# Expert rows summed on VectorE instead of TensorE, in a two-layer hybrid backbone with a product-key expert stage

## The chip, the cores and the metric

The kernel runs on one core of a Trainium2 chip. The metric is the device time of one execution in microseconds. The core has five instruction streams that run beside each other and meet at semaphores: TensorE (PE, with its weight loads PEld), VectorE (DVE), ScalarE (ACT), GpSimd (POOL) and SyncE (SP).

## The reference

The reference is one inference step over two layers for 128 prompt tokens and 512 sample tokens, 640 in all, with 1024 channels, in fp32. Each layer mixes tokens (three mixers and an attention) and then channels. The change touches only the second half of the channel mixing, the expert retrieval:

```python
s = jnp.einsum('thsk,snk->thsn', q, sub_keys)            # 8 heads, 2 sides, 128 keys
sv, si = lax.top_k(s, PEER_TOPK)                          # best 16 of each side
cand_s = sv[..., 0, :, None] + sv[..., 1, None, :]        # 256 sums
top_s, top_pos = lax.top_k(cand_s, PEER_TOPK)             # best 16 of them -> idx, g = softmax(top_s)

def block(args):                                          # 128 tokens, 128 experts a token
    tb, ib, gb = args
    a = jax.nn.gelu(jnp.einsum('tkd,td->tk', jnp.take(u_tab, ib, axis=0), tb))
    return jnp.einsum('tk,tkd->td', gb * a, jnp.take(v_tab, ib, axis=0))
```

So each token has 8 x 16 = 128 experts. For each, a row U of 1024 numbers is fetched and multiplied with the token (a dot product), the result goes through gelu and is weighted with the gate g, and a row V of 1024 numbers, scaled by that weight, is added to the token's output. Both tables hold 16,384 rows a layer, in device memory.

## The kernel before, in words

**Tiles.** The 640 tokens are five tiles of 128, one token a partition. In the expert stage, tile after tile, GpSimd fetches for expert n of all 128 tokens at once one U row each and one V row each by an indirect DMA: 128 x 4 KB = 512 KB a gather, 256 gathers a tile, 1280 a layer, 1342 MB in the whole kernel.

**Slots.** Four slots hold U rows and four hold V rows (`rows_u`, `rows_v`, in the ring that holds the weights in other stages). A gather waits until the slot is free (`rows_u_free`, `rows_v_free`; `gather`, L1600). GpSimd works in order: first the 16 U rows of a tile's first head, then U row n and V row n-16 in turn (`later_heads`, L1618), because the weight of a V row is only known when its head's 16 dot products are done. The last V rows of a tile are mixed with the first U rows of the next. The tile's indices stand in one buffer, `idx_u`; the last head's are copied to `idx_last` (`pass_last`), and the next tile's are put into `idx_u` (`pass_indices`, L1439) once VectorE has seen the V rows before them come in.

**VectorE** does a dot product per expert (`dot_products`, L1510; a multiply and sum of 128x1024 and a read of the accumulator). After 16 of them it drains and signals ScalarE, which takes the gelu of the 16 values (L1087). VectorE then builds 16 diagonal matrices for the head before (`diagonals`, L1498): the identity times activation times gate, 128x128 each, with two sets of 16 for two heads. Between groups of four dot products it does a part of the selection for the next tile (`select_part`, L1458: best keys of two heads at a time, pair sums, best sums, positions, indices, gates), in heads 2 to 7 of a tile. In the last tile of a layer there is no following one, and so no selection.

**TensorE** multiplies each diagonal with its V row and accumulates all 128 experts of a tile in PSUM, in two halves of 512 columns (L822); fp32 makes two passes of each, so four matmul records a row. At the end of the tile ScalarE copies the sum to SBUF, TensorE turns it (eight transposes, L830), and VectorE adds it, times the gate g2, to the residual (`add_output`, L1488). TensorE also computes the next tile's key scores and turns the next tile's tokens, from a staging buffer that ScalarE fills.

**Order.** The instructions of each engine are written out by hand. PSUM accumulators are handed on in a fixed order of turns (`turn_table`, L81). The layers are a hardware loop on every engine, and so are most tiles; inside such a loop the value of a wait is computed in registers.

Of the kernel before, what the change touches and what calls it, by code (L numbers as in the profile page):

```python
# [75 lines left out]
ROWS_U, ROWS_V = 4, 4  # L76
LAST = EXPERTS - TOPK
# [3 lines left out]
def turn_table():  # L81
# [8 lines left out]
    order += [("pq", n) for n in range(2 * PH)] + [("key", 0), ("key", 1), "tok"]  # L90

    for j in range(TILES - 1):
        names = [("next_key", 0), ("next_key", 1), "next_tok", "peer_out"]
        order += names if j == 0 else [(name, j) for name in names]
    order += ["peer_last"]
# [55 lines left out]
def build(nc, x_prompt, x_sample, cache_ckv, cache_kpe, c, c_ctx, w_ada, b_ada, norm1, norm2, w_in,  # L151
# [4 lines left out]
    with ExitStack() as ctx:  # L156
# [44 lines left out]
        g2_cur = sb("g2_cur", [P, KC])  # L201
# [42 lines left out]
        pq_t = view(0, 2 * PH, T)  # L244
# [19 lines left out]
        idx_u, idx_v = kt_flat[:, 0:P].bitcast(U32), kt_flat[:, 4 * P:5 * P].bitcast(U32)  # L264
        g_cur = kt_flat[:, P:2 * P]
        dots, acts = kt_flat[:, 2 * P:3 * P], kt_flat[:, 3 * P:4 * P]
        idx_last = idx_v[:, 0:TOPK]
        idx_next, g_next = kt_flat[:, 5 * P:6 * P].bitcast(U32), kt_flat[:, 6 * P:7 * P]
        ring_flat = ring[:].rearrange("p s n -> p (s n)")
        rows_u = ring_flat[:, 0:ROWS_U * D].rearrange("p (s n) -> p s n", s=ROWS_U)  # L270
        rows_v = ring_flat[:, ROWS_U * D:(ROWS_U + ROWS_V) * D].rearrange("p (s n) -> p s n", s=ROWS_V)
        diag = [m_flat[:, n * TOPK * P:(n + 1) * TOPK * P].rearrange("p (k n) -> p k n", k=TOPK) for n in range(2)]
        tok_cur = m_flat[:, 4096:4096 + D]
        stage = cv_flat[:, 2048:2048 + D].rearrange("p (k n) -> p k n", k=KC)
        y_tok = uq[:].rearrange("p k h n -> p (k h n)")[:, 0:D]
# [71 lines left out]
        last_ready = signal("last_ready", TILES)  # L347
        tok_ready = signal("tok_ready", TILES)
        stage_ready = signal("stage_ready", 3 * (TILES - 1))
        y_full = signal("y_full", TILES)  # L350
# [6 lines left out]
        diag_ready = signal("diag_ready", TILES * PH)  # L357
        ytok_ready = signal("ytok_ready", TILES)
# [19 lines left out]
        def _(sp):  # L378
# [18 lines left out]
            with sp.Fori(0, LAYERS) as l:  # L397
# [41 lines left out]
        def _(pe):  # L439
# [62 lines left out]
            with pe.Fori(0, LAYERS) as l:  # L502
# [278 lines left out]
                def key_scores(name, n, more, queries):  # L781

                    a = open_turn(l, name, more)
                    for g in range(PH):
                        mm = pe.matmul(a[:, g * P:(g + 1) * P], queries[:, g, :], turned[:, 4 + g % 2, :],  # L785
                                       start=True, stop=True)
                    close_turn(name, mm)

                def tokens(name, more, tile):

                    a = open_turn(l, name, more)
                    for k in range(KC):
                        mm = pe.transpose(a[:, k * P:(k + 1) * P], tile[:, k, :], ident)
                    close_turn(name, mm)

                for n in range(2):
                    key_scores(("key", n), n, 0, pq_t[:, n * PH:(n + 1) * PH, 0:P])
                tokens("tok", 0, h_t[:, :, 0:P])

                def staged(j, n):  # L800

                    pe.wait_ge(stage_ready.sem, stage_ready.after(l, n + 1) + j * 3)

                def peer_tile(j, out, more, following):


                    for h in range(PH):
                        if following and h < 2:
                            staged(j, h)
                            key_scores(("next_key", h), h, j * 2, stage)  # L810
                        if following and h == H_TOK + 1:
                            staged(j, 2)
                            tokens("next_tok", j * 2, stage)
                        pe.wait_ge(diag_ready.sem, diag_ready.after(l, h + 1) + j * PH)
                        for k in range(TOPK):
                            n = h * TOPK + k
                            s = n % ROWS_V
                            pe.wait_ge(rows_v_in[s].sem,
                                       rows_v_in[s].after(l, 16 * (n // ROWS_V + 1)) + j * (16 * EXPERTS // ROWS_V))
                            for half in range(2):  # L820
                                cols = slice(half * 512, (half + 1) * 512)
                                mm = pe.matmul(y_acc[:, cols], diag[h % 2][:, k, :], rows_v[:, s, cols],  # L822
                                               start=n == 0, stop=n == EXPERTS - 1)
                            mm.then_inc(rows_v_free.sem, 1)
                    pe.drain().then_inc(y_full.sem, 1)
                    a = open_turn(l, out, more)

                    pe.wait_ge(ytok_ready.sem, ytok_ready.after(l, 1) + j)
                    for k in range(KC):
                        mm = pe.transpose(a[:, k * P:(k + 1) * P], y_tok[:, k * P:(k + 1) * P], ident)  # L830
                    close_turn(out, mm)

                with pe.Fori(0, TILES - 1) as j:
                    peer_tile(j, "peer_out", j * 2, True)
                peer_tile(TILES - 1, "peer_last", 0, False)
# [21 lines left out]
        def _(act):  # L857
# [40 lines left out]
            with act.Fori(0, LAYERS) as l:  # L898
# [151 lines left out]
                with act.Fori(0, 2) as i:  # L1050
                    for n in range(8):
                        a = full(l, ("pq", n), i * 4)
                        act.copy(arena[:, bass.ds(i * (8 * T) + n * T, T)], a[:, 0:T]).then_inc(pq_ready.sem, 1)
                        act.wait_ge(pq_ready.sem, pq_ready.after(l, n + 1) + i * 8)
                        act.sem_inc(give_back(("pq", n)), 1)

                def soft(j):

                    act.wait_ge(soft_in.sem, soft_in.after(l, 1) + j)
                    act.activation(best_e, best_e, ACT.Exp).then_inc(soft_exp.sem, 1)  # L1060

                def take_tokens(name, more, j):

                    a = full(l, name, more)
                    act.copy(tok_cur, a[:, 0:D]).then_inc(tok_ready.sem, 1)
                    act.wait_ge(tok_ready.sem, tok_ready.after(l, 1) + j)
                    act.sem_inc(give_back(name), 1)

                def put_stage(src):
                    act.copy(stage, src).then_inc(stage_ready.sem, 1)  # L1070

                def queries(j, n):

                    return pq_t[:, n * PH:(n + 1) * PH, bass.ds(j * P, P)]

                def peer_tile(j, following):
                    for h in range(PH):
                        if following and h == 0:
                            put_stage(queries(j + 1, 0))
# [42 lines left out]
        def _(dve):  # L1122
# [28 lines left out]
            with dve.Fori(0, LAYERS) as l:  # L1151
# [306 lines left out]
                def select_part(j, h, quarter):  # L1458
# [26 lines left out]
                    elif at == (6, 3):  # L1485
                        gates(j + 1)
# [245 lines left out]
```

## Time and profile before

| | |
|---|---|
| three executions, us | 6154.2, 6157.3, 6170.8; median 6157.3 |
| span of the profiled execution, us | 6172.5 |
| time of the profiled execution itself | not recorded apart from these; its span lies at the slowest of the three |
| busy: PE, PEld, DVE, ACT, POOL, us | 4637.5, 2050.5, 2873.5, 450.7, 2863.0 |
| read from device memory | 1484 MB, of which the gathers 1342 MB |
| mean granted TensorE clock | 0.938 |

Times in the rows are microseconds from the start of the span, unless marked ns; L12 is line 12 of the kernel before. An engine's busy time holds no register, branch or semaphore work and no waiting. GpSimd's gathers are busy while their descriptors are made; the transfers themselves then run on 16 DMA engines. The ends of matmuls are modelled. In a timeline, the bracket at the end of a row is the time for which the engine was idle before it, and what ended that.

### The profile page before, as it was taken

The numbers are of one execution on the slowest core, as the hardware profiler recorded it, in microseconds if no ns is written. First come the engines' busy times: TensorE is split into PE (matmuls) and PEld (weight loads), VectorE is DVE, ScalarE is ACT, GpSimd is POOL, SyncE is SP. The second block draws the span as 40 slices with busy tenths as digits, with TensorE's granted clock in tenths as the row PEclk, the third lists the DMA queues.
The fourth block names the chain that finished last, engine by engine and source line by source line (L and its number), as shares of the span: only waits on it lengthen the run. The fifth ranks groups of instructions, "written<-read, shape, count | busy, mean of one in ns | idle before, by whom it ended". The sixth has DMA issues, their size and how long they took to land.

```text
span 6172.5 us, 45021 instructions
## 1 busy us (share of the span) xinstructions
PE 4637.5 (75%) x12847; PEld 2050.5 (33%) x12847; DVE 2873.5 (47%) x6890; ACT 450.7 (7%) x830; POOL 2863.0 (46%) x2569
## 2 busy tenths in 40 slices
PE   7999996566666766667789999956676766666666
PEld 3645544122222222222245555532222222222222
DVE  2241113665656656545312411146657566565543
ACT  1131010000000000000010400100000000000000
POOL 0000000676776767777500000017767777677774
PEclk9999998899999999999999999978999999999999
DMA  7101110899999999999851012119999999999996
GB/s 231 55 28 36 60 55 14 318 346 340 339 353 330 337 333 331 348 332 368 310 170 63 21 43 66 48 45 325 352 343 333 339 329 339 340 335 354 345 354 245
DMA packets 504201, 1489.50 MB, mean 241 GB/s; under 512 B 49632, under 2 KB 172976, under 8 KB 502578
## 3 DMA queue, kind: packets, MB, share of 16 engines
q0 software_dynamic: 368640, 1342.34, 59.6%
q1 hardware_dynamic: 126000, 140.54, 7.1%
q10 hardware_dynamic: 9346, 4.38, 0.3%
q8 instruction: 58, 0.95, 0.1%
q14 instruction: 157, 1.29, 0.1%
HBM read 1484.30 MB, written 2.79 MB: 241 GB/s over the span
## 4 chain that ended last, share of the span: by engine, by line
PE 39%; DMA 24%; issue 18%; DVE 9%; POOL 7%; ACT 1%; DVEq 1%; POOLq 0%; another core or an unknown queue 0%; PEldq 0%; PEld 0%; ACTq 0%; SPq 0%
DMA ring<-in_peer_v_dram,kt 16%; PE ps L468 10%; PE ps L822 10%; DMA ring<-in_peer_u_dram,kt 7%; POOL ring L1605 7%; PE ps L747 7%; DVE m_t L1506 3%; PE ps L511 2%; PE ps L754 2%; DVE ring L1517 2%; PE ps L552 1%; PE ps L699 1%; PE ps L679 1%; PE ps L627 1%; PE ps L499 1%
## 5 line engine op out<-in xcount | busy, mean ns | idle before, releaser
L822 PE MATMUL ps<-ring,m_t 128*128 128x512 f32 x5120 | 2655.2, 651 | 1270.3 <-DMA ring<-in_peer_v_dram,kt 913.1
L1605 POOL DMA_INDIRECT ring<-in_peer_u_dram,kt x1280 | 1363.8, 1065 | 2742.0 <-issue 1447.6
L1517 DVE CUSTOM_DVE_ANT_0 ring<-ring,m_t 128x1024 f32<-128x1024 f32 x1280 | 1553.7, 1225 | 1465.9 <-DMA ring<-in_peer_u_dram,kt 1403.3
L822 PEld LDWEIGHTS ps<-ring,m_t 128*128 128x128 f32 x5120 | 940.1, 201 | 2969.5 <-DMA ring<-in_peer_v_dram,kt 1797.0
L1605 POOL DMA_INDIRECT ring<-in_peer_v_dram,kt x1280 | 1498.6, 1171 | 519.1 <-issue 286.3
L468 PE MATMUL ps<-h_t,ring 128*128 128x128 f32 (+1 forms) x1536 | 426.1, 438 | 21.9 <-ACT h_t L895 14.6
L747 PE MATMUL ps<-h_t,ring 128*128 128x128 f32 (+1 forms) x1536 | 425.1, 435 | 11.7 <-issue 9.1
L1506 DVE TENSOR_SCALAR m_t<-cst,kt 128x128 f32<-128x128 f32 x1280 | 343.8, 367 | 21.5 <-issue 11.6
L468 PEld LDWEIGHTS ps<-h_t,ring 128*128 128x128 f32 x1536 | 235.1, 192 | 214.6 <-issue 209.7
L747 PEld LDWEIGHTS ps<-h_t,ring 128*128 128x128 f32 x1536 | 235.4, 191 | 199.6 <-issue 199.6
L1087 ACT ACTIVATE kt<-kt 128x16 f32<-128x16 f32 x80 | 17.3, 216 | 3439.7 <-DVEq L1533 1905.6
L511 PE MATMUL ps<-ring,cond_t 128*2 128x256 f32 x768 | 176.3, 383 | 31.9 <-issue 19.5
L1337 DVE TENSOR_TENSOR arena<-arena,ps 128x512 f32<-128x512 f32 x64 | 28.3, 484 | 336.6 <-ACT arena L1043 336.6
L1361 DVE MAX8 zc<-ps 128x8 f32<-128x128 f32 x160 | 38.2, 286 | 307.5 <-PE ps L785 290.1
L468 PE MATMUL ps<-m_t,ring 128*128 128x128 f32 (+1 forms) x512 | 143.8, 442 | 7.6 <-DVEq L1341 6.1
L511 PEld LDWEIGHTS ps<-ring,cond_t 128*2 128x2 f32 x768 | 62.4, 85 | 145.2 <-issue 56.0
L754 PE MATMUL ps<-cv,ring 128*128 128x128 f32 (+1 forms) x384 | 109.1, 434 | 0.0
L552 PE MATMUL ps<-ring,h_t 128*128 128x256 f32 (+1 forms) x480 | 98.5, 366 | 14.0 <-ACT h_t L895 14.0
L1156 DVE COPY arena<-ps 2x256 f32 x48 | 19.8, 412 | 186.0 <-PE ps L511 186.0
L1517 DVE DVE_READ_ACCUMULATOR2_ANT kt<- 128x1 f32 x1280 | 105.6, 83 | 0.0
L468 PEld LDWEIGHTS ps<-m_t,ring 128*128 128x128 f32 x512 | 79.1, 193 | 72.4 <-issue 72.4
L1337 DVE TENSOR_TENSOR m_t<-arena,ps 128x512 f32 (+1 forms) x32 | 14.2, 484 | 187.1 <-ACT arena L1043 187.1
(212 smaller groups left out, 2592.1 us busy)
## 6 DMA issues: line engine op xcount, KB each, us to landing
ring<-in_w_ada_dram SPq DMA_DIRECT2D x48, 1024.0 KB, 6.7
ring<-in_w_in_dram SPq DMA_DIRECT2D x36, 1024.0 KB, 5.4
ring<-in_peer_u_dram,kt POOLq DMA_INDIRECT x1280
ring<-in_peer_v_dram,kt POOLq DMA_INDIRECT x1280
ring<-in_peer_wq_dram SPq DMA_DIRECT2D x16, 1024.0 KB, 5.5
ring<-in_tables_dram SPq DMA_DIRECT2D x10, 1024.0 KB, 4.8
ring<-in_w_out_dram SPq DMA_DIRECT2D x8, 1024.0 KB, 5.0
ring<-in_w_branch_c_dram SPq DMA_DIRECT2D x8, 512.0 KB, 6.5
```

The lines of the kernel that those rows point to most:

```text
L468: mm = pe.matmul(a[:, lo:hi], lhs[k], rhs[k][:, lo:hi], start=k == 0, stop=k == n - 1)
L499: mm = pe.matmul(a[:, lo:hi], mean_w[:], m_t[:, k, lo:hi], start=k == 0, stop=k == KC - 1)
L511: mm = pe.matmul(a[0:2, 0:CW], cond_t[:, 0:2, k], w[:, k, :], start=k == 0, stop=k == KC - 1)
L552: mm = pe.matmul(a[:, at:at + n], h_t[:, k, j * P:(j + 1) * P], w[:, k, 0:n], start=k == 0, stop=k == KC - 1)
L627: mm = pe.matmul(a[:, at:at + 512], big[:, j, q * P:(q + 1) * P], hy[:, j, lo:lo + 512], start=j == 0, stop=j == STILES - 1)
L679: mm = pe.matmul(a[:, at:at + hi - lo], q_t[:, h, j * P:(j + 1) * P], k_h[h % 2][:, lo:hi], start=True, stop=True)
L747: pe.matmul(a[:, at_g:at_g + hi - lo], wg[:, k, cols], h_t[:, k, lo:hi], start=k == 0, stop=k == KC - 1)
L754: mm = pe.matmul(a[:, at_y:at_y + hi - lo], wb[:, (0, 2, 4)[b] + k, cols], y_k[b][k][:, lo:hi], start=k == 0, stop=k == n - 1)
L822: mm = pe.matmul(y_acc[:, cols], diag[h % 2][:, k, :], rows_v[:, s, cols], start=n == 0, stop=n == EXPERTS - 1)
L1506: ins = dve.tensor_scalar(diag[h % 2][:, k, :], ident, acts[:, n:n + 1], g_cur[:, n:n + 1], ALU.mult, ALU.mult)
L1517: dve.tensor_tensor_reduce(rows_u[:, s, :], rows_u[:, s, :], tok_cur, 1.0, 0.0, ALU.mult, ALU.add, dots[:, n:n + 1]).then_inc(rows_u_free. ...
L1605: pool.indirect_dma_start(rows[:, s, :], None, table, bass.IndirectOffsetOnAxis(ap=idx, axis=0)).then_inc(came[s].sem, 16)
```

## The change

It does five things.

1. The weighted sum of V rows moves to VectorE. `diagonals` and the matmuls with them go. `make_weights` multiplies activation and gate for a head; `add_row` waits for a V row, does `y = row * weight + y` over 128x1024 in SBUF, drains, and frees the slot. `add_row` of expert n-16 stands directly before the dot product of expert n. The sum is complete in SBUF, so ScalarE's copy of it goes too; TensorE still turns it.
2. There are eight V slots in place of four; the new four stand where the diagonals were.
3. Indices and gates have two buffers, by the parity of the tile; `pass_indices` and `pass_last` go, with the wait for V rows.
4. The tile loops and the layer loops are unrolled on all engines; waits have constants. GpSimd goes straight on from one tile to the next.
5. ScalarE's staging copies go, since TensorE can address every tile's data directly; for this the queries `pq_t` are laid out by tile. The output addition of a tile stands in the next tile after the second quarter of its fourth head, no longer after its first head.

```diff
-ROWS_U, ROWS_V = 4, 4
+ROWS_U, ROWS_V = 4, 8
...
-                def diagonals(j, h):
-                    if h >= 2:
-                        dve.wait_ge(rows_v_free.sem, rows_v_free.after(l, (h - 1) * TOPK) + j * EXPERTS)
-                    dve.wait_ge(acts_ready.sem, acts_ready.after(l, h + 1) + j * PH)
-                    for k in range(TOPK):
-                        n = h * TOPK + k
-                        ins = dve.tensor_scalar(diag[h % 2][:, k, :], ident, acts[:, n:n + 1],
-                                                g_cur[:, n:n + 1], ALU.mult, ALU.mult)
-                    ins.then_inc(diag_ready.sem, 1)
+                def make_weights(j, h):
+                    cols = slice(h * TOPK, (h + 1) * TOPK)
+                    dve.wait_ge(acts_ready.sem, acts_ready.after(l, j * PH + h + 1))
+                    dve.tensor_tensor(wts[:, cols], acts[:, cols], g_of[j % 2][:, cols], ALU.mult)
+                    dve.drain()
+
+                def add_row(j, n):
+                    s, y = n % ROWS_V, y_sums[:, j % 2, :]
+                    dve.wait_ge(rows_v_in[s].sem, rows_v_in[s].after(l, 16 * ((j * EXPERTS + n) // ROWS_V + 1)))
+                    if n == 0:
+                        dve.tensor_scalar(y, rows_v[s], wts[:, n:n + 1], None, ALU.mult)
+                    else:
+                        dve.scalar_tensor_tensor(y, rows_v[s], wts[:, n:n + 1], y, ALU.mult, ALU.add)
+                    last = dve.drain()
+                    last.then_inc(rows_v_free.sem, 1)
+                    if n == EXPERTS - 1:
+                        dve.sem_inc(y_ready.sem, 1)
...
                 def dot_products(j, h, k0, k1):
                     for k in range(k0, k1):
                         n = h * TOPK + k
+                        if n >= TOPK:
+                            add_row(j, n - TOPK)
+                        elif j:
+                            add_row(j - 1, n + EXPERTS - TOPK)
                         s = n % ROWS_U
...
+                for j in range(TILES):
+                    dve.wait_ge(tok_ready.sem, tok_ready.after(l, j + 1))
+                    for h in range(PH):
+                        if h:
+                            make_weights(j, h - 1)
+                        elif j:
+                            make_weights(j - 1, PH - 1)
+                        for quarter in range(4):
+                            if j + 1 < TILES:
+                                select_part(j + 1, h, quarter)
+                            dot_products(j, h, quarter * TOPK // 4, (quarter + 1) * TOPK // 4)
+                            if j and (h, quarter) == (3, 1):
+                                add_output(j - 1)
+                        dve.drain().then_inc(dots_ready.sem, 1)
+                make_weights(TILES - 1, PH - 1)
+                for n in range(EXPERTS - TOPK, EXPERTS):
+                    add_row(TILES - 1, n)
+                add_output(TILES - 1)
...
+                for j in range(TILES):
+                    for n in range(EXPERTS):
                         u_row(j, n)
+                        if n >= TOPK:
+                            v_row(j, n - TOPK)
+                        elif j:
+                            v_row(j - 1, n + EXPERTS - TOPK)
+                for n in range(EXPERTS - TOPK, EXPERTS):
+                    v_row(TILES - 1, n)
```

## Rows read from the trace of the kernel before

**Rows 1.** The page's slices: busy share of the DMA engines in tenths, 154 us each.
```profile
DMA  7101110899999999999851012119999999999996
```
**Rows 2.** The page's chain of waits, shares of the span by engine.
```profile
PE 39%; DMA 24%; issue 18%; DVE 9%; POOL 7%; ACT 1%; DVEq 1%; POOLq 0%; another core or an unknown queue 0%; PEldq 0%; PEld 0%; ACTq 0%; SPq 0%
```
**Rows 3.** Busy time by stretches: one steady tile of the first layer.
```profile
core 0: us, PE busy (x) PEld busy (x) DVE busy (x) ACT busy (x) POOL busy (x), PEclk, DMA share, GB/s
1458.00:1849.00 391.00, 267.68 (x558) 97.65 (x559) 243.05 (x599) 12.11 (x18) 285.17 (x255) 0.95 0.93 341
```
**Rows 4.** Groups by line, 1458 to 1849 us: busy us, mean ns; idle before.
```profile
L1605 POOL DMA_INDIRECT ring<-in_peer_v_dram,kt x127 | 149.2, 1175 | 47.4 <-issue 30.4 <-PE ps L822 13.5 <-remote 3.5
L1605 POOL DMA_INDIRECT ring<-in_peer_u_dram,kt x128 | 136.2, 1064 | 58.4 <-issue 33.8 <-DVE kt L1517 20.1 <-PE ps L822 4.5
L1506 DVE TENSOR_SCALAR m_t<-cst,kt 128x128 f32<-128x128 f32 x115 | 31.0, 369 | 2.0 <-issue 1.2 <-ACT kt L1087 0.7
```
**Rows 5.** Timeline of GpSimd: start, us, what, idle before.
```profile
1710.59 2.66 POOL L1605 DMA_INDIRECT ring<-in_peer_v_dram,kt  x1 [0.30 <-issue]
...
1716.16 1.98 POOL L1605 DMA_INDIRECT ring<-in_peer_v_dram,kt  x1 [0.30 <-issue]
...
1734.40 0.94 POOL L1605 DMA_INDIRECT ring<-in_peer_v_dram,kt  x1 [0.30 <-issue]
```
**Rows 6.** Timeline of VectorE at the same time, columns alike.
```profile
1710.15 2.28 DVE L1413 TENSOR_TENSOR cv<-zc,cst 128x2048 f32<-128x2048 f32 x1
1712.67 1.23 DVE L1517 CUSTOM_DVE_ANT_0 ring<-ring,m_t 128x1024 f32<-128x1024 f32 x1 [0.23 <-issue]
...
1714.97 1.22 DVE L1517 CUSTOM_DVE_ANT_0 ring<-ring,m_t 128x1024 f32<-128x1024 f32 x1
...
1716.12 1.22 DVE L1517 CUSTOM_DVE_ANT_0 ring<-ring,m_t 128x1024 f32<-128x1024 f32 x1
```
**Rows 7.** Timeline of VectorE around two drains, one with an increment.
```profile
629.12 0.89 DVE L1337 TENSOR_TENSOR arena<-arena,ps 128x512 f32<-128x512 f32 x2 [11.64 <-ACT arena L1043]
630.12 0.83 DVE L1340 TENSOR_TENSOR m_t<-m_t,arena 128x640 f32 x1
...
1079.09 2.29 DVE L1428 TENSOR_REDUCE zc<-cv 128x128 f32<-128x2048 f32 x1
1081.45 0.29 DVE L1433 SCALAR_TENSOR_TENSOR zc<-zc 128x128 f32<-128x128 f32 x1
```
**Rows 8.** Timeline of VectorE: the first instruction of four tiles.
```profile
1083.79 0.23 DVE L1524 COPY kt<-kt 128x128 f32<-128x128 f32 x1 [0.55 <-issue]
...
1458.45 0.33 DVE L1524 COPY kt<-kt 128x128 f32<-128x128 f32 x1
...
2652.52 0.23 DVE L1524 COPY kt<-kt 128x128 f32<-128x128 f32 x1
...
5716.30 0.23 DVE L1524 COPY kt<-kt 128x128 f32<-128x128 f32 x1
```
**Rows 9.** Timeline of VectorE: the first op after the first head.
```profile
1118.01 0.17 DVE L1537 COPY g_cur<-g_all 128x8 f32<-128x8 f32 x1
```
**Rows 10.** Timeline of VectorE: parts of the selection.
```profile
1047.64 0.29 DVE L1376 CAST zc<-zc 128x256 f32<-128x256 uint32 x1
...
1512.67 0.48 DVE L1361 MAX8 zc<-ps 128x8 f32<-128x128 f32 x2
...
1515.58 1.21 DVE L1517 CUSTOM_DVE_ANT_0 ring<-ring,m_t 128x1024 f32<-128x1024 f32 x1
```
**Rows 11.** Timeline of all engines at the second layer's end.
```profile
6092.99 0.08 DVE L1517 DVE_READ_ACCUMULATOR2_ANT kt<- 128x1 f32 x1
...
6093.47 4.26 DVE L1506 TENSOR_SCALAR m_t<-cst,kt 128x128 f32<-128x128 f32 x16 [0.40 <-ACT kt L1087]
...
6134.06 2.16 DVE L1493 SCALAR_TENSOR_TENSOR x_t<-ps,g_cur,x_t 128x128 f32<-128x128 f32 x8 [36.33 <-PE ps L830]
...
6154.51 6.46 DVE L1583 SCALAR_TENSOR_TENSOR h_t<-x_t,cond_t,root 128x640 f32<-128x640 f32 x8
```

More of the change, by code:

```diff
@@ L89, in turn_table @@
     order += [("gate", n) for n in range(3 * KC)] + [("out", n) for n in range(KC)] + ["norm2"]
[L90 to L95, printed above, removed]
+    order += [("pq", n) for n in range(2 * PH)] + [("key0", 0), ("key1", 0), ("tok", 0)]
+    for j in range(TILES):
+        if j + 1 < TILES:
+            order += [("key0", j + 1), ("key1", j + 1)]
+        if j:
+            order += [("peer_out", j - 1)]
+        if j + 1 < TILES:
+            order += [("tok", j + 1)]
+    order += [("peer_out", TILES - 1)]
     assert len(order) % 2 == 0, len(order)
@@ L395, in cols_of @@
                 return w[l, :, bass.ds(start, n)].rearrange("(k p) n -> p k n", p=P)
-            with sp.Fori(0, LAYERS) as l:
+            for l in range(LAYERS):
                 with sp.Fori(0, N_ADA // SLOTS) as i:
@@ L500, in root_mean @@
                 close_turn(name, mm)
-            with pe.Fori(0, LAYERS) as l:
+            for l in range(LAYERS):
                 pe.wait_ge(cond_ready, 2)
@@ L786, in key_scores, with tokens @@
                                        start=True, stop=True)
                     close_turn(name, mm)
-                def tokens(name, more, tile):
-                    a = open_turn(l, name, more)
+                def tokens(j):
+                    a = open_turn(l, ("tok", j))
                     for k in range(KC):
[L793 to L797, printed above, removed]
@@ L896, in add_shift @@
                                    bias=mod[:, shift + k, 1:2], scale=amp[:, which, k, 1:2]).then_inc(h_ready.sem, 1)
-            with act.Fori(0, LAYERS) as l:
+            for l in range(LAYERS):
                 def put(dst, src):
@@ L1049, in _ @@
                 add_shift(l, KC, 3 * KC)
[L1050 to L1055, printed above, removed]
+                for n in range(2 * PH):
+                    a = full(l, ("pq", n))
+                    act.copy(pq_t[:, :, n, :], a[:, 0:T].rearrange("p (j n) -> p j n", j=TILES))\
+                        .then_inc(pq_ready.sem, 1)
+                    act.wait_ge(pq_ready.sem, pq_ready.after(l, n + 1))
+                    act.sem_inc(give_back(("pq", n)), 1)
@@ L1149, in normalise @@
                     dve.tensor_tensor(h_t[:, k, :], x_t[:, k, :], rinv[:, :], ALU.mult).then_inc(scaled.sem, 1)
-            with dve.Fori(0, LAYERS) as l:
+            for l in range(LAYERS):
                 with dve.Fori(0, N_ADA // SLOTS) as i:
@@ L1350, in _, with best_keys @@
                 normalise(l, 1)
[L1353 to L1355 removed]
+                def best_keys(j, n, g0, g1):
+                    name = (f"key{n}", j)
+                    a = full(l, name)
                     carry_waits(dve, "dve")
@@ L1598, in _ @@
             pool.sem_inc(rows_v_free.sem, ROWS_V)
-            def gather(rows, idx, free, came, table, l, j, n, slots):
-                s = n % slots
-                pool.wait_ge(free.sem, free.after(l, n + 1 - slots) + j * EXPERTS)
-                carry_waits(pool, "pool")
-                pool.indirect_dma_start(rows[:, s, :], None, table, bass.IndirectOffsetOnAxis(
-                    ap=idx, axis=0)).then_inc(came[s].sem, 16)
             u_rows, v_rows = (w.rearrange("l n d -> (l n) d") for w in (peer_u, peer_v))
-            with pool.Fori(0, LAYERS) as l:
+            for l in range(LAYERS):
```

233 lines of the change are left out of this document (73 added, 160 removed).

## The prediction

> **What bounds the kernel now.** The slices of the page come first: the DMA digits stand at 9 in two long stretches, slices 9 to 19 and 28 to 39, and nowhere else for long [rows 1]. These are the expert stages of the two layers; the change works there. The chain of waits gives 39% to TensorE, 24% to DMA, 18% to "issue" [rows 2]: no engine owns the end, so the stage has to be read from inside.
>
> The table by stretches shows a tile with a following tile: 391 us hold 285.2 us of GpSimd in 255 gathers, 243 of VectorE, 268 of TensorE; DMA share 0.93 at 341 GB/s [rows 3]. Each gather has 0.30 us of "issue" ahead of it [rows 5], so GpSimd is occupied for 285.2 + 255 x 0.30 = 362 of 391 us. It is the nearest thing to a bound, with the DMA engines behind it. A gather of V rows takes 1.175 us in the mean and one of U rows 1.064 [rows 4], 2.84 us a pair with the issue time. Its shortest form is 0.94 [rows 5]; the long ones have a cause that can be read. The gather at 1710.59 took 2.66 us and VectorE's two-input op had begun at 1710.15 and ended at 1712.43; the one at 1716.16 took 1.98 under a dot product ending at 1717.34 [rows 5, 6]. Both end 0.8 us after the VectorE op does: a gather that starts under a VectorE op with two SBUF inputs is held until that op ends. The diagonals, with one tensor input, are 0.369 us each and 31 us of that stretch [rows 4].
>
> The cadence: tiles open at 1083.8, 1458.5 and 2652.5 (three tiles between the last two, 398.0 us each), and in the second layer the last one at 5716.3 [rows 8]. The last tile has no selection in it and takes until 6093.1, so 376.8 us, 47.1 us a head; then 43.1 us pass to the end of the last output addition (6134.06 + 2.16) [rows 8, 11].
>
> **The change part by part.**
>
> *Removed*: 1280 x 4 fp32 matmul passes on TensorE, off the path except at the end, and 128 diagonals a tile, 31 to 34 us of VectorE [rows 4] in a VectorE that now idles 148 of 391 us [rows 3].
>
> *Added*: on VectorE, for every expert, a multiply-add of 128x1024 and a drain. The nearest row is the dot product, same size, two SBUF inputs: 1.22 us, and 1.15 from start to start when nothing holds it (1714.97 to 1716.12) [rows 6]. The final scaling, the same operation at 640 columns, takes 6.46/8 = 0.81 us [rows 11], which fits one element per 1.04 ns. I take 1.22. The gap after a drain is 0.07 us alone (1081.38 to 1081.45), 0.11 with a semaphore increment (630.01 to 630.12) [rows 7], and 0.24 where a wait with a register value follows (1712.43 to 1712.67) [rows 6]. The new drain has an increment, and a wait on a constant behind it: 0.17, between the last two. So add 1.39, dot 1.15, **2.54 us a pair**; bounds 2.48 and 2.61.
>
> A head of 16 pairs costs 40.6 us, and 0.8 for its weights: the last dot of a head to VectorE's next instruction is 0.40 us, by way of ScalarE [rows 11], plus one small op and two drains. 41.4 us.
>
> *Selection* is as before but now lies in a VectorE without slack. Two heads of key scores take 1512.67 to 1515.58, 2.9 us, eight times a tile [rows 10]; the rest takes 35.6 us (1047.64 to 1083.24) [rows 8, 10]. By heads: 11.6 in the second and third, 12.5 in the fourth, 7.1, 9.5 and 6.5 in the next three. The output addition (2.2 us and drains, 2.6) falls into the fourth.
>
> A head is then the longer of VectorE's work and the supply of rows. For the supply I take the last tile's 47.1 us a head (2.9 us a pair), the only stretch without selection. The lower bound is VectorE's own pace; the upper is under rival B.
>
> - Steady tile: 47.1 + 53.0 + 53.0 + 56.5 + 50.6 + 50.9 + 49.5 + 47.1 = 407.7 (the fifth and seventh are 48.5 and 47.9 of VectorE, and 2.1 and 1.6 for their last pairs, which outrun the supply); plus 1.9 for the hand-over (the wait for the turned tokens, today behind the last diagonals); less 4, the rows landed ahead when the seventh head ends. 405.6 against 398.0: +7.6, three times, **+22.8**.
> - First tile: 34.2 for the U rows alone (1083.8 to 1118.0 [rows 8, 9]), then 53.0, 53.0, 53.9, 50.6, 50.9, 49.5, 43.1 and 1.9: 390.1 against 374.7. **+15.4**.
> - Last tile: supply, no change. **0**, between -33 (rival C) and +34 (rival B).
> - Tail: today 43.1 us, in which TensorE works off 16 rows at its own pace. Then: weights 0.8, 16 x 1.39 = 22.2, eight transposes on a cold TensorE and the hand-overs 2.3, the addition 2.2: 27.5. **-15.6**.
>
> Sum: +22.6 a layer, **+45 us**. The profiled execution has a span of 6172.5 us and lies at the top of the three times (6154 to 6171), so its rows may be 0.2% long; I set the sum on the median 6157 and get 6202, in round numbers **6200 us**.
>
> *Edits priced at nothing.* Eight V slots: GpSimd issues U row n+4 and then V row n-12 in order, and U row n+4 waits for dot n. When it waits there, the adds stand at n-16, so four V rows are out and the other four slots are unused; they matter only in the tail, where V rows run ahead. Unrolling: the same instructions run, with constants in place of register values; its only price is in the drain gap above. Double-buffered indices take away a lull at each hand-over (a wait for the last V rows); it is in the supply's spare time as long as VectorE is the longer, and if it is not, it gives back up to 3 us a tile. The pq copies go to strided places, once a layer, and the staging copies of ScalarE go: both beside other work.
>
> The Trainium skill speaks against this change: "SBUF — State Buffer", in its text on the shared port pair and on "DVE blocks DMA", says that VectorE with two SBUF inputs locks out a GpSimd op that reads SBUF, and that a gather's descriptors wait meanwhile. The trace agrees (0.8 us after the op's end, above); by it, what it leads to is rival B. The same page lets a one-input op in a two-port mode lock too; the diagonals are the candidates here, and gathers that begin under them are not visibly held. "VectorE: DVE Perf Modes", section on the DRAIN that can't be avoided, finds that semaphores after each op cost nothing extra; by that a pair would be 2.30 us and the steady tile some 20 us shorter. Rows 6 and 7 show 0.07 to 0.24 beyond the op's end, so I go by them.
>
> **The rivals.**
>
> *B, slower: GpSimd loses to the port.* Today the 128 dots cover 128 x 1.22 = 156 of 391 us, 40%, and the gathers are 0.18 us over 0.94 in the mean [rows 4], so some 0.4 where one is hit, the selection's long ops left aside. With adds, two-input ops cover 2.44 of 2.9 us, 84%. Hit at random, a gather pays 0.84 x 0.4 = 0.34, a pair 2 x (0.94 + 0.30 + 0.34) = 3.16 us, 51.3 us a head with the weights. This decides as soon as it exceeds the 47.1 above. Steady tile 423 (four heads at 51.3 or a little over, the rest as above), first 404, last 411, tail 27.5: 2112 against 374.7 + 1194 + 376.8 + 43.1 = 1989 a layer, +123, in all **6400 us**. Against it: a held gather goes through at the next op boundary, 0.8 + 0.3 us later the next one starts, and an op lasts 1.15 to 1.39. So GpSimd may fall into step, one gather for each VectorE op, and then costs nothing over 2.54 a pair. Both held gathers of the rows let the current op end and no further one [rows 5, 6].
>
> *C, faster: the supply improves.* Without the lull, in step, with the drain gap at 0.11 (pair 2.48) and rows every 2.64 us (400 GB/s): a head without selection takes 43.0 us and VectorE's own 40.5. Steady 391 (-7, three times), first 380 (+5), last 344 (-33), tail 26 (-17). That is 66 us a layer less, **6025 us**. For it: GpSimd unhindered needs 2.48 a pair. Against: the stretches never show more than 341 GB/s.
>
> *D, the slots do it:* if eight V slots really deepened the queue, the supply would be better than in C but VectorE's own sum for a steady tile (8 x 41.4 + 58.8 + 2.6 + 1.9 = 394.5) would still stand; nearly C's time, and counted there.
>
> **How the numbers follow.** Forecast (VectorE and the supply near balance, 6200, own range 6145 to 6260): 0.48. B (6260 to 6400 and over): 0.23. C (6020 to 6140): 0.27. Left over 0.02. About 0.3% (18 us) is what can be told from no change. Faster by more: all of C and a little of the forecast's lower end, 0.29. Same: 0.15. Slower: 0.56. The range 6050 to 6370 leaves out the ends of B and C.
>
> **What would show it.** Right: the multiply-add at 1.22 us and its successor 0.17 later; VectorE above 85% busy in heads with selection, its idle time in the first, last and light heads waiting for DMA; tiles at 405; tail 27. B: gathers at 1.3 us and longer in the mean, steady tiles over 415, VectorE idle in every head. C: DMA share over 0.95, last tile under 360. Wrong altogether: a drain that costs more than 0.3 us (each 0.1 is 10 us a tile), or an add over 1.3.

## The result, and the profile after

The changed kernel takes **6275.1 us** (median of four runs, 6267.6 to 6281.8), the kernel before 6155.8 (four runs): ratio **1.0213** [1.0179 to 1.0246]. The forecast was 6200, so the sign was right and the size was not: +119 us in place of +45. The spans of the two profiled executions, 6280.0 and 6172.5, differ by 107.5.

The page after: busy times, the DMA digits of the 40 slices, the chain's shares, and three groups (busy us, mean ns | idle before). They answer to [rows 1, 2, 4].

```profile
PE 2023.4 (32%) x7727; PEld 1142.2 (18%) x7727; DVE 4134.0 (66%) x6930; ACT 393.5 (6%) x779; POOL 2811.5 (45%) x2569
...
DMA  7101110899899898899951011118998998989997
...
DVE 35%; PE 29%; issue 15%; POOL 12%; DMA 6%; DVEq 2%; ACT 1%; POOLq 0%; PEldq 0%; PEld 0%; SPq 0%; ACTq 0%
...
L1547 POOL DMA_INDIRECT ring<-in_peer_u_dram,kt x1280 | 1441.4, 1126 | 3002.2 <-DVE kt L1392 2165.9
L1476 DVE CUSTOM_DVE_ANT_0 ring<-ring,m_t 128x1024 f32<-128x1024 f32 x1280 | 1568.0, 1225 | 233.7 <-issue 202.3
L1460 DVE SCALAR_TENSOR_TENSOR uq<-m_t,kt,uq 128x1024 f32<-128x1024 f32 x640 | 820.5, 1282 | 88.0 <-DMA m_t<-in_peer_v_dram,kt 78.1
```

VectorE's share of the chain goes from 9% to 35%, that of DMA from 24% to 6%: an engine that was hardly on the path now has the largest part of it. The DMA digits, all 9 inside the two expert stages before, fall to 8 in part. A multiply-add (L1460) lasts 1.282 us.

The timeline of VectorE in a steady tile, then GpSimd's beside it (start, us, what, idle before).

```profile
1603.04 1.28 DVE L1460 SCALAR_TENSOR_TENSOR uq<-m_t,kt,uq 128x1024 f32<-128x1024 f32 x1
1604.48 1.23 DVE L1476 CUSTOM_DVE_ANT_0 ring<-ring,m_t 128x1024 f32<-128x1024 f32 x1 [0.16 <-issue]
1605.63 0.08 DVE L1476 DVE_READ_ACCUMULATOR2_ANT kt<- 128x1 f32 x1
1605.63 1.28 DVE L1460 SCALAR_TENSOR_TENSOR uq<-m_t,kt,uq 128x1024 f32<-128x1024 f32 x1
```

```profile
1603.93 1.20 POOL L1547 DMA_INDIRECT ring<-in_peer_u_dram,kt  x1 [3.01 <-DVE kt L1476]
1605.44 1.08 POOL L1556 DMA_INDIRECT ring<-in_peer_v_dram,kt  x1 [0.30 <-issue]
1606.82 0.94 POOL L1547 DMA_INDIRECT ring<-in_peer_u_dram,kt  x1 [0.30 <-issue]
1608.06 1.04 POOL L1556 DMA_INDIRECT ring<-in_peer_v_dram,kt  x1 [0.31 <-issue]
1609.41 0.94 POOL L1547 DMA_INDIRECT ring<-in_peer_u_dram,kt  x1 [0.30 <-issue]
```

From add to add are 2.59 us, of which 0.16 behind the drain. From U gather to U gather are also 2.59 (1606.82 to 1609.41): GpSimd has fallen into step, one gather for each VectorE operation, and few are held for long: between 1500 and 1860 us 134 of 222 gathers last over 1.00 us, 8 of them over 1.7. All 134 end 0.80 to 0.82 us after the end of a VectorE operation. So what the prediction read from two gathers holds for all of them.

Busy time by stretches: a steady tile, then the last tile of the first layer; they answer to [rows 3].

```profile
core 0: us, PE busy (x) PEld busy (x) DVE busy (x) ACT busy (x) POOL busy (x), PEclk, DMA share, GB/s
1490.00:1880.00 390.00, 7.72 (x32) 6.63 (x32) 354.31 (x594) 4.38 (x10) 260.44 (x243) 0.50 0.91 324
2740.00:3090.00 350.00, 1.94 (x8) 1.57 (x8) 297.29 (x371) 1.51 (x7) 271.39 (x238) 0.50 0.97 357
```

VectorE is busy 91% of the steady stretch (62% before), and the core moves 324 GB/s there (341 before). TensorE's granted clock reads 0.50, the lower of its two levels (1.2 GHz), with 7.7 us of work in 390; nothing waits for it but the end of a tile.

The first dot products of tiles 1, 2, 3 and 5 and the tail of the first layer, on VectorE and TensorE; they answer to [rows 8, 11].

```profile
1088.50 1.23 DVE L1476 CUSTOM_DVE_ANT_0 ring<-ring,m_t 128x1024 f32<-128x1024 f32 x1 [4.58 <-DMA ring<-in_peer_u_dram,kt]
...
1485.63 1.23 DVE L1476 CUSTOM_DVE_ANT_0 ring<-ring,m_t 128x1024 f32<-128x1024 f32 x1 [0.16 <-issue]
...
1897.30 1.22 DVE L1476 CUSTOM_DVE_ANT_0 ring<-ring,m_t 128x1024 f32<-128x1024 f32 x1 [0.16 <-issue]
...
2727.62 1.23 DVE L1476 CUSTOM_DVE_ANT_0 ring<-ring,m_t 128x1024 f32<-128x1024 f32 x1 [0.16 <-issue]
...
3102.29 0.18 DVE L1449 TENSOR_TENSOR kt<-kt 128x16 f32<-128x16 f32 x1 [0.33 <-ACT kt L1050]
3102.55 5.50 DVE L1460 SCALAR_TENSOR_TENSOR uq<-ring,kt,uq 128x1024 f32<-128x1024 f32 x4
...
3119.39 5.50 DVE L1460 SCALAR_TENSOR_TENSOR uq<-m_t,kt,uq 128x1024 f32<-128x1024 f32 x4
...
3127.14 2.16 DVE L1440 SCALAR_TENSOR_TENSOR x_t<-ps,g_all,x_t 128x128 f32<-128x128 f32 x8 [2.25 <-PE ps L797]
```

Steady tiles take 414.0 us each (1485.63 to 2727.62, three tiles) against 398.0 [rows 8]. The same reading for both kernels, first dot to first dot (the last tile to its last dot, 3101.95), first layer, in us:

| | before | after | difference | forecast |
|---|---|---|---|---|
| first tile | 375.3 | 397.1 | +21.8 | +15.4 |
| three steady tiles | 1195.5 | 1242.0 | +46.5 | +22.8 |
| last tile | 367.6 | 374.3 | +6.7 | 0 |
| tail, to the end of the output addition | 43.2 | 27.4 | -15.8 | -15.6 |

That is +59.2 (forecast +22.6); the second layer, read alike, gives +18.3, +42.4, +6.2 and -15.8, so +51.1. Both together are 110.3 us, beside 107.5 between the spans. The heads of tile 2 in us, first dot to first dot (the forecast's 1.9 for the hand-over is put to the first head, its "less 4" to the eighth):

```
before    52.5  51.5  47.9  49.1  48.6  47.8  46.9  51.9
forecast  49.0  53.0  53.0  56.5  50.6  50.9  49.5  43.1
after     48.8  54.2  54.1  56.7  50.5  51.6  47.6  48.1
```

Heads 2 to 6 came out within 1.2 us of the forecast; the seventh is 1.9 below it and the eighth 5.0 above.

What GpSimd waited for around the last tile of the first layer (us in total, times, longest):

```profile
POOL ring L1547 <- issue: 36.6, 120, 0.3
POOL ring L1556 <- issue: 20.6, 63, 1.7
POOL m_t L1556 <- issue: 19.5, 64, 0.3
POOL ring L1547 <- DVE kt L1476: 6.7, 4, 2.5
POOL ring L1556 <- DVE kt L1476: 0.8, 1, 0.8
```

Nearly all of it is the 0.30 us of issue ahead of each gather. In the stretch from 2740 to 3090 us shown above, GpSimd is occupied for 271.4 + 238 x 0.30 = 343 of 350 us, and waits some 7 us for free slots. Its gathers take 1.14 us in the mean, 0.94 when nothing holds them. VectorE in turn waits 48 times for a V row there, 30 us in all.

### The profile page after: what moved, and what is told of

Same layout as the page of the kernel before. It is cut to its first block, busy times and chain, and to the rows that moved or that the text cites. A ratio compares the mean times of both kernels' runs of the same rounds, so it can differ in the third digit from the quotient of the medians.

```text
span 6280.0 us, 32515 instructions
## 1 busy us (share of the span) xinstructions
PE 2023.4 (32%) x7727; PEld 1142.2 (18%) x7727; DVE 4134.0 (66%) x6930; ACT 393.5 (6%) x779; POOL 2811.5 (45%) x2569
## 4 chain that ended last, share of the span: by engine, by line
DVE 35%; PE 29%; issue 15%; POOL 12%; DMA 6%; DVEq 2%; ACT 1%; POOLq 0%; PEldq 0%; PEld 0%; SPq 0%; ACTq 0%
DVE uq L1460 13%; DVE ring L1476 12%; PE ps L463 10%; POOL ring L1547 9%; PE ps L742 7%; DMA m_t<-in_peer_v_dram,kt 3%; PE ps L749 2%; PE ps L506 2%; POOL ring L1556 2%; POOL m_t L1556 1%; PE ps L547 1%; DMA ring<-in_peer_v_dram,kt 1%; PE ps L694 1%; DVE zc L1347 1%; PE ps L622 1%
## 5 line engine op out<-in xcount | busy, mean ns | idle before, releaser
L1547 POOL DMA_INDIRECT ring<-in_peer_u_dram,kt x1280 | 1441.4, 1126 | 3002.2 <-DVE kt L1392 2165.9
L1460 DVE SCALAR_TENSOR_TENSOR uq<-m_t,kt,uq 128x1024 f32<-128x1024 f32 x640 | 820.5, 1282 | 88.0 <-DMA m_t<-in_peer_v_dram,kt 78.1
L1460 DVE SCALAR_TENSOR_TENSOR uq<-ring,kt,uq 128x1024 f32<-128x1024 f32 x630 | 807.6, 1282 | 81.5 <-DMA ring<-in_peer_v_dram,kt 71.3
L1556 POOL DMA_INDIRECT ring<-in_peer_v_dram,kt x640 | 688.5, 1076 | 209.5 <-issue 207.4
L1556 POOL DMA_INDIRECT m_t<-in_peer_v_dram,kt x640 | 680.9, 1064 | 209.0 <-issue 206.3
L781 PE MATMUL ps<-turned,arena 128*128 128x128 f32 x320 | 67.9, 399 | 1736.7 <-ACTq L1043 1461.0
L797 PE MATMUL ps<-cst,uq 128*128 128x128 f32 x80 | 19.6, 426 | 1848.5 <-DVEq L1464 1335.3
L781 PEld LDWEIGHTS ps<-turned,arena 128*128 128x128 f32 x320 | 63.0, 302 | 1742.4 <-ACTq L1043 1463.2
L797 PEld LDWEIGHTS ps<-cst,uq 128*128 128x128 f32 x80 | 15.7, 223 | 1851.8 <-issue 1336.8
L506 PE MATMUL ps<-ring,cond_t 128*2 128x256 f32 x768 | 175.4, 382 | 30.7 <-issue 15.4
L789 PE MATMUL ps<-cst,h_t 128*128 128x128 f32 x80 | 19.7, 428 | 510.6 <-DVEq L1085 510.6
```

Source lines behind the costliest of these rows:

```text
L506: mm = pe.matmul(a[0:2, 0:CW], cond_t[:, 0:2, k], w[:, k, :], start=k == 0, stop=k == KC - 1)
L781: mm = pe.matmul(a[:, g * P:(g + 1) * P], pq_t[:, j, n * PH + g, :], turned[:, 4 + g % 2, :], start=True, stop=True)
L1460: dve.scalar_tensor_tensor(y, rows_v[s], wts[:, n:n + 1], y, ALU.mult, ALU.add)
L1547: pool.indirect_dma_start(rows_u[s], None, u_rows, bass.IndirectOffsetOnAxis(ap=idx_u[j % 2][:, n:n + 1], axis=0)).then_inc(rows_u_in[s].s ...
L1556: pool.indirect_dma_start(rows_v[s], None, v_rows, bass.IndirectOffsetOnAxis(ap=idx_u[j % 2][:, n:n + 1], axis=0)).then_inc(rows_v_in[s].s ...
```

## The experiments

**Theories**, with the numbers that the expectations use. 1: VectorE's own sum sets the tiles, and its add and drain are dearer than priced. 2: the supply of rows is what VectorE waits for, and the slots, GpSimd held at the port (the prediction's rival B) or the DMA engines set it. 3, named first with the run of eight U slots (e6): four U slots are too few to keep the rows coming while VectorE does a burst of other work, such as the selection. "Port" stands for the shared port pair that the prediction speaks of. The runs are called e1 to e11. Each ratio is to the kernel before, run on the same chip.

**The changed kernel again** (e9).

> The changed kernel itself, beside the two below on one chip, as the measure for the other experiments. All theories: 2.1% over the kernel before, as in its own comparison.

Measured 1.0221 [1.0203 to 1.0239], tiles 396.3, 411.5, 414.3, 414.0, 372.7, tail 27.3. The result stands.

**The drain behind each add taken away** (e1). A wait for the add before it stands ahead of each add instead.

```diff
+                    dve.wait_ge(rows_v_free.sem, rows_v_free.after(l, j * EXPERTS + n))
...
-                        dve.scalar_tensor_tensor(y, rows_v[s], wts[:, n:n + 1], y, ALU.mult, ALU.add)
-                    last = dve.drain()
-                    last.then_inc(rows_v_free.sem, 1)
+                        ins = dve.scalar_tensor_tensor(y, rows_v[s], wts[:, n:n + 1], y, ALU.mult, ALU.add)
+                    ins.then_inc(rows_v_free.sem, 1)
```

> Changed kernel; the drain after each multiply-add is replaced by a semaphore increment on the multiply-add itself and a wait for it ahead of the next one, a dot product later. Theory 1 (VectorE's serial time sets the tiles with selection): the 0.16 us gap behind every add goes, a pair takes 2.43 instead of 2.59 us, 2.6 us a head in the five heads a tile that VectorE holds at 50 to 57 us, 13 us a tile, eight such tiles: about 105 us less than the changed kernel, 6170 us. Theory 2 (the supply of rows, by slots and by GpSimd held at the port, sets them): under 25 us less, 6250 or more.

Measured 1.0165 [1.0149 to 1.0182], 6229.8 us: some 0.5% better, a third of what the pairs alone promise. VectorE, and GpSimd in the same tile:

```profile
1604.97 1.28 DVE L1461 SCALAR_TENSOR_TENSOR uq<-ring,kt,uq 128x1024 f32<-128x1024 f32 x1
1606.17 1.22 DVE L1477 CUSTOM_DVE_ANT_0 ring<-ring,m_t 128x1024 f32<-128x1024 f32 x1
1607.31 0.08 DVE L1477 DVE_READ_ACCUMULATOR2_ANT kt<- 128x1 f32 x1
1608.04 1.28 DVE L1461 SCALAR_TENSOR_TENSOR uq<-ring,kt,uq 128x1024 f32<-128x1024 f32 x1 [0.65 <-DMA ring<-in_peer_v_dram,kt]
```

```profile
1568.80 0.93 POOL L1557 DMA_INDIRECT ring<-in_peer_v_dram,kt  x1 [0.31 <-issue]
1570.04 1.96 POOL L1548 DMA_INDIRECT ring<-in_peer_u_dram,kt  x1 [0.30 <-issue]
...
1577.45 1.99 POOL L1557 DMA_INDIRECT ring<-in_peer_v_dram,kt  x1 [0.30 <-issue]
```

The dot product now starts 1.20 us after the add's start, not 1.44, so a pair is 2.34. But VectorE then waits for rows, 35 of 225 gathers between 1500 and 1860 us last over 1.7 us (8 of 222 in the changed kernel), and the mean over all rises from 1.10 to 1.17. So the port is a real limit. Of the 35 long gathers 17 began less than 0.1 us before an add's end, when the dot product had already begun, and ended 0.81 us after that dot product's end; the one at 1570.04 is an example. In the changed kernel, where the drain keeps the two operations apart, none of the eight long ones is of this kind.

**Four V slots in place of eight** (e2; `ROWS_U, ROWS_V = 4, 4`).

> Changed kernel with four V slots instead of eight. Theory 1 and the argument that GpSimd, in order behind U row n+4, never has more than four V rows out: no change in the tiles, up to 5 us a layer lost in the tail, 6275 to 6285. Rival (the eight slots deepen the queue): 20 us or more slower, over 6295.

Measured 1.0271 [1.0254 to 1.0289], 6294.3 us, more than was expected and just under the rival's 6295. Yet the tiles are as in the changed kernel (410.5, 414.2 and 411.4 for the steady ones, last 369.3), and the tails are 36.3 and 35.2 in place of 27.4 and 27.3. The eight slots act only where forecast, in the tail, but give 8 to 9 us a layer there: with four, adds wait up to 2.7 us for their row. The traces thus show 17 us of the 0.5% (31 us) between this ratio and e9's; the rest is within the two intervals.

**The selection left out of both kernels** (e3 the changed kernel, e4 the one before). In tiles 2 to 5 of each layer the best keys, pair sums, positions and indices are left out; each tile uses the indices of the first.

```diff
+                        dve.tensor_copy(idx_u[j % 2], idx_u[(j - 1) % 2]).then_inc(idx_ready.sem, 1)
```

> Changed kernel; the selection for the second to fifth tile of each layer is left out (they take the first tile's indices and gates). Theory 1: every tile falls to the last tile's 375 us from 412 to 415, the first by 25: some 145 us a layer, 5985 us. Theory 2 (supply sets the tiles): the selection is beside the supply, and under 60 us go in all.

> Kernel before, with the same selection left out. Theory 1 says that VectorE had 140 us of slack a tile there, so little is gained: heads fall from 48 or 49 to the last tile's 46, 10 us a tile, some 80 us in all, 6075. If selection were on the path in both kernels alike: 290 us less, 5865.

Measured 0.9767 [0.9747 to 0.9787] for the changed kernel and 0.9742 [0.9725 to 0.9758] for the one before. A stretch of a steady tile, changed kernel first:

```profile
1500.00:1800.00 300.00, 7.41 (x32) 6.42 (x32) 255.95 (x324) 4.17 (x9) 231.43 (x204) 0.51 0.96 355
```

```profile
1500.00:1800.00 300.00, 220.22 (x448) 80.46 (x448) 156.98 (x316) 5.21 (x10) 227.82 (x210) 0.96 0.98 367
```

The changed kernel's ratio is 5987 us, where theory 1 expected 5985. Without the selection the two ways of summing nearly cost the same. The surprise is the other half. The kernel before gains 161 us where 55 were expected: its steady tiles fall from 398 to some 375 in the first layer and 369 in the second, although VectorE had 148 of 391 us idle [rows 3]. So the selection held up the supply in the kernel before too.

**The kernel before, with loops unrolled and double-buffered indices** (e5), sum still on TensorE, four slots each.

```diff
-                with dve.Fori(TILES - 2, TILES - 1) as j:
-                    peer_tile(j + 1, j, False)
+                for j in range(TILES):
+                    peer_tile(j, j - 1 if j else None, j + 1 < TILES)
...
-                    idx, at = (idx_u, n) if n < LAST else (idx_last, n - LAST)
-                    gather(rows_v, idx[:, at:at + 1], rows_v_free, rows_v_in, v_rows, l, j, n, ROWS_V)
+                    gather(rows_v, idx_u[j % 2][:, n:n + 1], rows_v_free, rows_v_in, v_rows, l, j, n, ROWS_V)
```

> Kernel before with the unrolling and the double-buffered indices and gates of the change alone; the sum stays on TensorE, four and four slots. Theory 1: the change's cost is VectorE's alone, so this part is level or a little better: 3 us less at each of eight hand-overs, 6105 to 6130 against 6130. Rival (the unrolled code or the lost copies cost something): over 6150.

Measured 0.9945 [0.9923 to 0.9967], 6104.3 us. This part of the change is a gain of 0.5%. Against it, the four-slot run e2 gives what the sum costs: 1.0271 / 0.9945 = 1.033, so 3.3% at four slots each. e5 still has the staging copies that the change drops; e10 below, without them, gives 1.0271 / 0.9935 = 1.034.

**The changed kernel with eight U and seven V slots** (e6), the new ones in space that is free in this stage.

```diff
-ROWS_U, ROWS_V = 4, 8
+ROWS_U, ROWS_V = 8, 7
```

> Changed kernel with eight U and seven V slots (the others lie in the used-up queries and in the conv buffer). Theory 1 (VectorE's serial sum is the bound in tiles with selection): a tile falls from 412 to that sum, 128 x 2.59 + 59 + 11 = 402, the first as much; some 40 us a layer, 6180. Theory 3 (bursts of VectorE work empty four U slots and the DMA engines stand still) says the same for the heads without selection and also that the DMA share rises in them. If neither the slots nor the bursts matter: 6260.

Measured **0.9918** [0.9891 to 0.9946], 6089.8 us, 90 less than expected. A steady tile, then the last:

```profile
1500.00:1850.00 350.00, 7.72 (x32) 6.62 (x32) 325.06 (x561) 4.38 (x10) 231.90 (x219) 0.50 0.90 327
2720.00:2980.00 260.00, 0.00 (x0) 0.00 (x0) 241.39 (x309) 1.29 (x6) 197.64 (x196) 0.50 1.01 393
```

Tiles 382.6, 399.8, 398.9, 399.2, last 337.1. The last is 42.1 us a head, and 16 x 2.59 + 0.8 is 42.2: VectorE's own sum, with no wait for rows. With it a steady tile should take 8 x 42.2 + 58.8 + 2.6 + 1.9 = 400.9, and takes 399.3. The same core moves 393 GB/s where the changed kernel moves 357. So the 47 us a head that I had taken for the supply of rows was not the limit of the DMA engines. It came with the four U slots (e2 shows that the V slots are not it), but hardly as waiting for a slot, which was some 7 of 350 us in the changed kernel and is 4 of 260 here. What changed is how long gathers are held: beyond 0.94 us each they lost 48 of 350 us in the changed kernel and lose 15 of 260 here, mean 1.14 against 1.02. VectorE no longer waits for a row in this stretch (48 times before), its operations follow in an even rhythm, and GpSimd stays in step with it. Why deeper U slots lead to this was not tested by itself.

**The same without the drain** (e7).

> The same slots, and the drain after each multiply-add replaced by a semaphore as in e1. Theory 1 + 3: e1 gained only 31 us because the slots' depth then set the pace; with the slots a steady tile takes 128 x 2.43 + 59 + 11 = 381 us, near the 375 of the stretches without selection: 6180 less 130 to 160, about 6030. Rival (gathers are held at the port once the gap behind the add is gone, and GpSimd's pace sets the tile): 6150 or more, mean gather over 1.15 us.

Measured 0.9902 [0.9871 to 0.9933], 6072.5 us: between the two expectations, with the gathers as long as the rival said, and not to be told from e6. The last tile's stretch:

```profile
2720.00:2980.00 260.00, 0.00 (x0) 0.00 (x0) 228.11 (x292) 1.25 (x6) 203.59 (x186) 0.50 0.99 375
```

Steady tiles gain 10 us (388.8, 391.6, 387.9) and the last one loses 18 (354.8 against 337.1): mean gather over the whole run 1.19 us against 1.05, and in this stretch 186 gathers against 196. GpSimd is occupied there for 203.6 + 186 x 0.30 = 259 of 260 us: it sets the pace. Where only pairs run back to back, the gap is worth more to GpSimd than its 0.24 us costs VectorE; in tiles with selection it is the reverse, perhaps because the selection's operations give gathers other openings, which was not tested.

**The sum on TensorE with six U and five V slots** (e8), on top of the unrolled kernel before; no staging copies. And as its control the same kernel with four and four (e10).

```diff
-ROWS_U, ROWS_V = 4, 4
+ROWS_U, ROWS_V = 6, 5
```

> Sum on TensorE as before; unrolled; no staging copies; six U and five V slots. Theory 3: the kernel before loses 20 us a tile because selection and diagonals come in bursts that four U slots don't cover; with six most of it comes back, tiles at 380 to 385, 5990 to 6030. If the bursts act otherwise (by holding gathers at the port): 6100.

> Sum on TensorE, unrolled, no staging copies, four and four slots: e8 with its slots taken back. Theory 3 (the slots carried e8's gain): like e5, ratio 0.99 to 1.00. Rival (the staging copies gone, or queries laid out by tile, carried it): near e8's 0.968.

Measured **0.9684** [0.9657 to 0.9712], 5947.5 us, with six and five, and 0.9935 [0.9910 to 0.9959], 6094.7 us, with four and four. The first is 43 us below the lower end of what was expected. The control equals the unrolled kernel e5, so the slots alone are worth 0.9684 / 0.9935, 2.5%. Steady tiles are 378.4, 378.8, 372.6 with the selection in them: the loss that the selection had made in the kernel before comes back with slots.

```profile
1500.00:1800.00 300.00, 216.34 (x440) 78.53 (x438) 202.92 (x507) 4.17 (x9) 237.67 (x204) 0.95 0.95 352
```

VectorE is idle for a third of this stretch. GpSimd is not: it is occupied for 237.7 + 204 x 0.30 = 299 of 300 us and waits 8 for slots (e10: 275, and 25 for slots). Here more slots do end a wait for slots, as theory 3 says, and GpSimd's own pace is then what is left. Against the VectorE sum with eight and seven, on the same chip, 6089.8 / 5947.5 is 1.024: with fewer slots the TensorE sum still wins.

**That version, with only the last head of each layer summed on VectorE** (e11), to keep the tail's gain.

```diff
+                    dve.wait_ge(ytok_ready.sem, ytok_ready.after(l, TILES))
+                    for n in range(LAST, EXPERTS):
...
+                        dve.scalar_tensor_tensor(y_tok, rows_v[s], wts[:, n - LAST:n - LAST + 1], y_tok,
+                                                 ALU.mult, ALU.add)
+                        dve.drain().then_inc(rows_v_free.sem, 1)
```

> e8, and in the last tile of each layer the last head's 16 V rows are added on VectorE into the sum that ScalarE has copied, in place of TensorE with diagonals. The tail of e8 is 37 us a layer; in the changed kernel 16 adds of 1.44 us and the turn made it 27. So 9 to 11 us a layer less, 20 us in all, ratio 0.965. Rival (the V rows, not the engine, set the tail in e8): no gain.

Measured 0.9683 [0.9663 to 0.9704], 5942.2 us: no gain that can be told. The tail is 33.4 us against 37.2, not 27:

```profile
2919.45 1.28 DVE L1533 SCALAR_TENSOR_TENSOR uq<-cv,kt,uq 128x1024 f32<-128x1024 f32 x1 [2.66 <-ACT uq L1087]
...
2928.42 1.29 DVE L1533 SCALAR_TENSOR_TENSOR uq<-ring,kt,uq 128x1024 f32<-128x1024 f32 x1 [0.67 <-DMA ring<-in_peer_v_dram,kt]
```

The adds wait 2.66 us for ScalarE's copy of the first 112 experts, and later up to 0.97 for V rows that five slots do not hold ready.

## Why the prediction was wrong in size

- **VectorE as the bound in heads with selection, right.** In tile 2's heads 2 to 6 (267 us) its idle time is the 0.16 us behind each drain, 13 us in all, and 3 us more. Without selection the loss is gone, as it had to be.
- **The tail, right** (27.4 for 27.5), though in part by luck: the 1.39 us from add to add were put together as 1.22 + 0.17, and the 1.40 measured there are 1.28 + 0.12.
- **Against the forecast the two layers are 65 us over** (110.3 for 45). Heads 2 to 6 of the eight tiles before the last are 38 us over, their seventh and eighth heads 24, the two last tiles 13. Some 9 us less come from the kernel before, which reads that much longer here, from first dot to first dot, than in the forecast. Three steps stand behind this.
- **"2.54 us a pair", the largest term that was mis-sized; it measured 2.59.** The step read 6.46 / 8 = 0.81 us at 640 columns as a duration. It is a spacing: in the trace of the kernel before one of the eight lasts 0.88 us and starts 0.80 after the one ahead of it. The add lasts 1.28 us, its drain 0.16 more: 1.44 for 1.39. That is 0.8 us in each head that VectorE bounds, in five heads of eight tiles 32 of the 38 us. The "VectorE: DVE Perf Modes" page of the Trainium skill, section on the DRAIN that can't be avoided, was read too quickly as being against the rows: it times a semaphore after each of eight copies, and no drain instruction. The run without the drain agrees with it (pair 2.34 with an increment on every add, 2 x 1.15 = 2.30 by the prediction's working). The explicit drain is what costs, 0.24 us.
- **"Less 4, the rows landed ahead when the seventh head ends", the step that failed.** The seventh head used that lead (47.6 us for the forecast's 49.5), and the eighth fell back to the pace of the rows, 48.1 for 43.1. Both together are 3 us a tile.
- **"47.1 us a head" as the supply, and "last tile: no change", failed too.** The size held in the changed kernel (46.8 a head), but by luck. It was not the pace of the kernel before: its last tile has one long first head (51.1) and 45.2 in the seven others; the change took away the first and slowed the rest, +6.7. Nor was it a property of the transfers. In the changed kernel it is GpSimd's pace with held gathers: 32 x (1.14 + 0.30) = 46 us a head. With eight U slots the gathers take 1.02 there and VectorE's own 42.1 us a head are left. The prediction asked what the eight V slots would do, and never asked this of the four U slots.
- **Rival B, rightly set against in size**: gathers 1.10 us in the mean, not 1.3, and in step where VectorE never waits. But its mechanism is at work in the heads that are not VectorE's: in the last tile gathers are held 48 of 350 us, and that is the pace. The Trainium skill, "SBUF — State Buffer", in its text on the shared port pair, has whoever comes first hold it for the whole instruction. The held gathers of 1.96 us in the run without the drain agree. The prediction took the waiting of a gather's descriptors from the same page as a consequence of two SBUF inputs; the page tells it of an op in a 2-port mode, and infers that a `tensor_tensor` leaves the making of descriptors alone. The trace of the kernel before shows gathers held under one (2.66 us under an op of 2.28), and it decides.
- **The two measures.** The medians lie 119 us apart and the spans 107.5, since the profiled execution of the kernel before was a long one (span 6172.5, median 6155.8), as the prediction had said of it.
- **Rival C, set against by a misreading.** That "the stretches never show more than 341 GB/s" is read from a tile with selection. The prediction's own 47.1 us a head are 128 x 2 x 512 KB in 376.8 us, 356 GB/s, and the last tile of the kernel before, below, moves 360. The supply that C asked for, rows every 2.64 us, was there with eight U slots.

```profile
2660.00:3025.00 365.00, 254.61 (x506) 90.73 (x505) 186.00 (x374) 2.52 (x8) 273.56 (x251) 0.95 0.97 360
```

What each part is worth, then: the sum on VectorE +3.3%, the unrolling with two index buffers -0.5%, eight V slots -0.3 to -0.5% (the tails alone; 1.0221 against 1.0271), net +2.2%.

**Open.** Why four U slots make the gathers of the changed kernel start at times at which they are held was not tested. With selection, the first head of a following tile in the first layer is long in the kernels that sum on TensorE (51 to 57 us, with deep slots too), and 42 to 51 in those that sum on VectorE. That it is the hand-over of the accumulator was not tested. More V slots for the last version's tail were not tried.

## What to carry to other kernels

Before work is moved to an engine with idle time, add up its serial chain in each stage, with the gap behind each drain, and compare it with the stage's cadence there: 38% idle over the stage was none in five of eight heads. Where a pace looks like that of the transfers, ask how many buffers stand behind it, and add up the engine that issues them (its busy time and the issue time ahead of each): here a DMA share of 0.92 to 0.97 hid that eleven slots for eight were worth 2.5%, and that GpSimd was occupied for 98% of the last tile. And time a change of buffer depth before a rearrangement of work, since each changes what the other seems worth.

## What the runs showed of the hardware

- A drain with an increment behind a multiply-add costs 0.24 us from start to start of the dot product behind it (1.44 against 1.20), 0.16 of it beyond the end of the operation. In the tail, from add to add, it is 1.40 against 1.32 with a semaphore.
- A gather that begins under a VectorE operation with two SBUF inputs is held: in the changed kernel all 134 of 222 gathers over 1.00 us end 0.80 to 0.82 us after a VectorE operation's end. One that misses an end, because the next operation has already begun, waits for that one too (1.96 us).
- GpSimd's gathers fit between such operations, one per operation, where each pair holds a gap of 0.16 us and VectorE does not wait for rows (mean 1.02 us in e6's last tile). Where it does, the mean is 1.14 with the gap (last tile of the changed kernel); over the whole runs it is 1.05 to 1.10 with the gap and 1.17 to 1.19 without.
- The DMA share is no scale for what more can be had: 0.97 at 357 GB/s with four U and eight V slots, 0.98 at 367 in the kernel before without selection, 1.01 at 393 with eight and seven.
